# Gate and up with the rows' low parts stacked into the stationary operand, and a fold matmul that sums the halves

## The chip, the cores and the metric

The kernel runs on one core of one Trainium2 chip. The metric is the time on the device in microseconds (us), from three runs of the kernel before; a profile of one further execution gives the rows below.

## The reference, cut to what matters

One layer of a decoder for 512 tokens of 1024 numbers, all in f32: a token mixing stage (retention and a gated linear recurrence), then a mixture of experts (MoE). Each token goes to 2 of 32 experts; an expert has a gate and an up matrix (1024 x 512 each) and a down matrix (512 x 1024).

```python
def expert_rows(args):
    xb, e = args
    h = jax.nn.silu(xb @ w_e_gate[e]) * (xb @ w_e_up[e])
    return h @ w_e_down[e]
```

The results of a token's two experts are weighted and added, and a layer norm ends the layer.

## The kernel before, in words

**Precision.** TensorE multiplies in fp32r, a form of f32 that it takes faster and with fewer bits. To keep more of them each operand is split: the high part is the value rounded to fp32r (a copy by ScalarE), the low part is what is left (a subtraction by VectorE). `products` (line 1402) then issues three matmuls for each block of 128 of the inner dimension: high x high, high x low, low x high (lines 1406, 1407, 1408), all into one PSUM bank.

**The MoE stage.** The kernel goes through the 32 experts in order, with up to 64 rows (tokens) of an expert at a time (`ROWS = 64`). Further rows of an expert are left to an overflow part at the end, which has nothing to do with these inputs. An expert's weights are six units of 1 MB each (128 partitions x 2048 f32): two halves each of gate, up and down, called G0, G1, U0, U1, D0, D1 here. A unit is loaded by SyncE's queue into one of 12 buffers (`m_raw`, `MRING = 12`), rounded by ScalarE into one of 3 buffers of `m_hi` (`m_hi_part`, line 787, which waits until TensorE has finished the unit three before), and completed by VectorE in `m_lo` (`m_lo_part`, line 1329), which also frees the load's buffer. SyncE issues a load when its buffer is free (line 381).

**The rows.** GpSimd gathers the rows of an expert from device memory into `xg` (line 492). TensorE turns them (`turn_x`, line 1618: eight transposes of 64 rows x 128 columns, line 1625), so that the inner dimension lies on the partitions, into PSUM (`bank_x`). ScalarE and VectorE split them into `xe_hi` and `xe_lo` (lines 795 and 1333). These have 128 columns, of which the 64 rows fill the first 64; the others were set to zero once (lines 815 to 817). They are the stationary operands of gate and up (`gate_up`, line 1628): 4 units x 4 blocks x 3 products = 48 matmuls with 512 moving columns, gate into bank 0 and up into bank 1. Only PSUM partitions 0 to 63 of the result mean anything.

**From gate and up to down.** ScalarE takes silu of the gate bank (`silu_part`, line 803, 128x512), VectorE multiplies it with the up bank into `h_sb` (`h_part`, line 1341, 128x512). TensorE turns h (`turn_h`, line 1639, four transposes), ScalarE and VectorE split it into `ht_hi` and `ht_lo` (lines 799 and 1337), and `down` (line 1646) makes 2 units x 2 blocks x 2 halves x 3 products = 24 matmuls into banks 2 and 3. ScalarE copies them out (`y_out`, line 807) and GpSimd scatters the rows to device memory.

**The order** is written out by hand for each engine, and each engine works strictly in its order. In the body for expert e (a loop of 15 turns with two experts in each, then once more for e = 30), with `hi` for `m_hi_part`, `lo` for `m_lo_part`, and 2 to 7 for U0, U1, D0, D1 and the next expert's G0 and G1:

```python
# TensorE, line 1665
gate_up(e + 1, u); turn_x(e + 2); down(e, u.ahead(4)); turn_h(e + 1)
# ScalarE, line 827
hi(2); ht_hi_part(e); hi(3); hi(4); silu_part(e + 1, ..); hi(5); hi(6); xe_hi_part(e + 2); hi(7); y_out(e, ..)
# VectorE, line 1355
lo(2); ht_lo_part(e); lo(3); lo(4); lo(5); h_part(e + 1, ..); lo(6); xe_lo_part(e + 2); lo(7)
```

So gate and up of the next expert run before down of this one. The waits are counts on semaphores: `m_done` (TensorE has finished a unit), `m_hi_ok` and `m_split_ok` (a unit's high part, both parts are there), `xe_turned`, `xe_split`, `m_silu`, `h_ok`, `h_turned`, `ht_hi_ok`, `ht_split`, `y_ok`. Ahead of the loop stand the first rows, and gate and up of expert 0 (lines 1660 to 1663, 812 to 825, 1346 to 1353); behind it down of expert 31 and the final norm. `Unit` (line 74) numbers the units and gives a unit's buffer. Elsewhere in the kernel the router (line 1580) multiplies in plain f32, eight matmuls with 128 stationary and 36 moving columns for each block of 128 tokens, and line 1573 transposes 128x128 blocks of f32.

Of the kernel before, what the change touches and what calls it, by code (L numbers as in the profile page):

```python
# [110 lines left out]
def layer(nc, io, out):  # L111
    ctx = ExitStack()
    with ctx:
# [56 lines left out]
        xe_hi, xe_lo = at("xe_hi", 128, [P, KD, P], F32R), at("xe_lo", 132, [P, KD, P], F32R)  # L170
        xg = at("xg", 136, [P, D])
        y_sb = at("y_sb", 140, [P, D])
        silu, h_sb = at("silu", 144, [P, FE]), at("h_sb", 146, [P, FE])
        ht_hi, ht_lo = at("ht_hi", 148, [P, FE // P, P], F32R), at("ht_lo", 150, [P, FE // P, P], F32R)
        bank_x = bank[:, 4:6, :].rearrange("p b (k n) -> p (b k) n", n=P)
        bank_h = bank[:, 6, :].rearrange("p (k n) -> p k n", n=P)
# [82 lines left out]
        m_silu, h_ok, h_turned, ht_hi_ok, ht_split = sem("m_silu"), sem("h_ok"), sem("h_turned"), sem("ht_hi_ok"), sem("ht_split")  # L259
# [313 lines left out]
        def _(act):  # L573
# [221 lines left out]
            def xe_hi_part(s):  # L795
                act.wait_ge(xe_turned, s + 1)
                copy(xe_hi[:, :, 0:ROWS], bank_x[:, :, 0:ROWS]).then_inc(xe_hi_ok, 1)

            def ht_hi_part(s):
                act.wait_ge(h_turned, s + 1)  # L800
                copy(ht_hi[:, :, 0:ROWS], bank_h[:, :, 0:ROWS]).then_inc(ht_hi_ok, 1)

            def silu_part(s, u):
                m_finished(u)
                act.activation(silu[:, :], bank[:, 0, :], ACT.Silu).then_inc(m_silu, 1)
# [9 lines left out]
            for tile in (xe_hi, xe_lo, ht_hi, ht_lo):  # L815
                n = tile.shape[1]
                act.activation(tile[:, :, ROWS:P], ident[:, 0:P - ROWS].unsqueeze(1).to_broadcast([P, n, P - ROWS]), ACT.Copy, scale=0.0)
# [3 lines left out]
            for j in range(4):  # L821
                if j == 2:
                    silu_part(0, u.ahead(1))
                m_hi_part(u.ahead(j + 2))
            xe_hi_part(1)

            def act_next(e, u):

                m_hi_part(u.ahead(2))
                ht_hi_part(e)  # L830
                m_hi_part(u.ahead(3))
                m_hi_part(u.ahead(4))
                silu_part(e + 1, u.ahead(1))
                m_hi_part(u.ahead(5))
                m_hi_part(u.ahead(6))
                xe_hi_part(e + 2)
                m_hi_part(u.ahead(7))
                y_out(e, u.ahead(5))

# [8 lines left out]
            with act.If(n_over > 0):  # L848
                with act.Fori(0, (MAX_OVERFLOW + 1) // 2) as i:
                    for b in range(2):  # L850
                        j = 2 * i + b
                        with act.If(n_over > j):
# [4 lines left out]
                            silu_part(j + EXPERTS, u.ahead(1))  # L857
# [19 lines left out]
        def _(dve):  # L877
# [448 lines left out]
            dve.tensor_scalar(lists_x[0:ROWS, :], lists[0:ROWS, :], 1, None, ALU.logical_shift_right).then_inc(lists_x_ok, 1)  # L1326

# [5 lines left out]
            def xe_lo_part(s):  # L1333
                dve.wait_ge(xe_hi_ok, s + 1)
                sub(xe_lo[:, :, 0:ROWS], bank_x[:, :, 0:ROWS], xe_hi[:, :, 0:ROWS]).then_inc(xe_split, 1)

            def ht_lo_part(s):
                dve.wait_ge(ht_hi_ok, s + 1)
                sub(ht_lo[:, :, 0:ROWS], bank_h[:, :, 0:ROWS], ht_hi[:, :, 0:ROWS]).then_inc(ht_split, 1)

            def h_part(s, u):
                dve.wait_ge(m_done, u.n + 1 + MSPLIT)
                dve.wait_ge(m_silu, s + 1)
                tt(h_sb[:, :], bank[:, 1, :], silu[:, :], ALU.mult).then_inc(h_ok, 1)
# [7 lines left out]
            h_part(0, u.ahead(3))  # L1352
            xe_lo_part(1)

            def dve_next(e, u):

                m_lo_part(u.ahead(2))
                ht_lo_part(e)
                for j in range(3, 6):
                    m_lo_part(u.ahead(j))  # L1360
                h_part(e + 1, u.ahead(3))
                m_lo_part(u.ahead(6))
                xe_lo_part(e + 2)
                m_lo_part(u.ahead(7))

# [6 lines left out]
            with dve.If(n_over > 0):  # L1372
                with dve.Fori(0, (MAX_OVERFLOW + 1) // 2) as i:
                    for b in range(2):
                        j = 2 * i + b
                        with dve.If(n_over > j):
# [4 lines left out]
                            h_part(j + EXPERTS, u.ahead(3))  # L1381
# [19 lines left out]
        def _(pe):  # L1401
# [216 lines left out]
            def turn_x(s, ahead=0):  # L1618
# [5 lines left out]
                for k in range(KD):  # L1624
                    last = pe.transpose(bank_x[:, k, 0:ROWS], xg[0:ROWS, P * k:P * k + P], ident[0:ROWS, 0:ROWS])  # L1625
                last.then_inc(xe_turned, 1)

            def gate_up(s, u):
                pe.wait_ge(xe_split, s + 1)
                for b in range(2):  # L1630
                    for half in range(2):
# [3 lines left out]
                        products(bank[:, b, :], [(xe_hi[:, 4 * half + k, :], xe_lo[:, 4 * half + k, :],  # L1635
                                                  m_hi[:, sl, FE * k:FE * k + FE], m_lo[:, sl, FE * k:FE * k + FE]) for k in range(4)],
                                 half == 0, half == 1).then_inc(m_done, 1)

            def turn_h(s):
                pe.wait_ge(h_ok, s + 1)  # L1640
                pe.sem_inc(marks, 1)
                for k in range(4):
                    last = pe.transpose(bank_h[:, k, 0:ROWS], h_sb[0:ROWS, P * k:P * k + P], ident[0:ROWS, 0:ROWS])  # L1643
                last.then_inc(h_turned, 1)
# [18 lines left out]
            turn_h(0)  # L1663

            def pe_next(e, u):
# [4 lines left out]
                turn_h(e + 1)  # L1670
# [8 lines left out]
            with pe.If(n_over > 0):  # L1679
                with pe.Fori(0, (MAX_OVERFLOW + 1) // 2) as i:  # L1680
                    for b in range(2):
                        j = 2 * i + b
                        with pe.If(n_over > j):
                            u = Unit(M_END + 6 * b, 0, i, 12, MRING)
                            turn_x(j + (EXPERTS + 1), 1)
                            gate_up(j + EXPERTS + 1, u)
                            turn_h(j + EXPERTS)
# [39 lines left out]
```

## Time and profile before

| | us |
|---|---|
| median of 3 runs | 1469.64 |
| lowest and highest | 1469.45, 1474.08 |
| span of the profiled execution | 1470.0 |
| TensorE busy in it | 1361.7 (93%) |
| VectorE busy | 956.6 (65%) |
| ScalarE busy | 780.9 (53%) |
| GpSimd busy | 205.4 (14%) |

The profiled execution has no time of its own beside its span, which runs from its first to its last instruction; it stands 0.4 us above the median. TensorE has two rows in the profile: PE is the matmuls and transposes, PEld their weight loads, which run beside them. A matmul with 512 moving columns shows some 0.39 us while the next begins 0.227 us after it, since they are pipelined: the distance of starts is what a matmul costs, not its duration. "fp32r" in a row is the split form; the names are the program's with buffer numbers left out. DVE is VectorE, ACT ScalarE, POOL GpSimd.

### The profile page before, as it was taken

The numbers are of one execution on the slowest core, as the hardware profiler recorded it, in microseconds if no ns is written. First come the engines' busy times: TensorE is split into PE (matmuls) and PEld (weight loads), VectorE is DVE, ScalarE is ACT, GpSimd is POOL, SyncE is SP. The second block draws the span as 40 slices with busy tenths as digits, with TensorE's granted clock in tenths as the row PEclk, the third lists the DMA queues.
The fourth block names the chain that finished last, engine by engine and source line by source line (L and its number), as shares of the span: only waits on it lengthen the run. The fifth ranks groups of instructions, "written<-read, shape, count | busy, mean of one in ns | idle before, by whom it ended". The sixth has DMA issues, their size and how long they took to land.

```text
span 1470.0 us, 18266 instructions
## 1 busy us (share of the span) xinstructions
PE 1361.7 (93%) x6264; PEld 1113.0 (76%) x6264; DVE 956.6 (65%) x1013; ACT 780.9 (53%) x768; POOL 205.4 (14%) x177
## 2 busy tenths in 40 slices
PE   7999999999999999999988089999999999999970
PEld 6888878878888888888877067777888888887860
DVE  5478853363734734634654368888888888888857
ACT  5676653223424333334321257777777777777751
POOL 0000000000000000003300312222222222222222
PEclk9999999999999999999998589999999999999995
DMA  7233213523131322332474369999999999999804
GB/s 225 81 90 102 71 58 97 164 74 113 58 114 58 100 85 72 100 86 72 129 272 162 142 212 351 367 370 376 361 357 372 366 370 367 366 374 365 322 13 171
DMA packets 202404, 294.20 MB, mean 200 GB/s; under 512 B 11968, under 2 KB 109424, under 8 KB 201856
## 3 DMA queue, kind: packets, MB, share of 16 engines
q1 hardware_dynamic: 196224, 283.17, 56.2%
q0 software_dynamic: 5568, 8.47, 1.7%
q10 hardware_dynamic: 576, 2.10, 0.4%
q8 instruction: 21, 0.34, 0.1%
q14 instruction: 15, 0.12, 0.0%
HBM read 289.96 MB, written 12.65 MB: 206 GB/s over the span
## 4 chain that ended last, share of the span: by engine, by line
PE 89%; DVE 4%; DMA 2%; ACT 2%; issue 2%; POOL 1%; ACTq 0%; POOLq 0%; DVEq 0%
PE bank L1406 29%; PE bank L1408 28%; PE bank L1407 28%; PE bank L1625 1%; PE bank L1643 1%; PE bank L1580 1%; DVE x L1394 1%; DVE wo_lo L885 1%; DMA list_dram<-val,addr 1%; DMA x_rows<-in_x_dram 0%; PE bank L1508 0%; DMA xg<-x_dram,x_idx 0%; DVE x L1193 0%; POOL list_dram L490 0%; DVE m_lo L885 0%
## 5 line engine op out<-in xcount | busy, mean ns | idle before, releaser
L885 DVE TENSOR_TENSOR m_lo<-m_raw,m_hi 128x2048 fp32r<-128x2048 f32 x192 | 439.4, 2289 | 93.5 <-ACT m_hi L575 93.5
L575 ACT ACTIVATE m_hi<-m_raw 128x2048 fp32r<-128x2048 f32 x192 | 368.1, 1918 | 112.2 <-PE bank L1408 111.7
L885 DVE TENSOR_TENSOR w_lo<-raw,w_hi 128x1024 fp32r<-128x1024 f32 x120 | 148.5, 1239 | 184.6 <-ACT w_hi L575 183.3
L1406 PE MATMUL bank<-xt_hi,w_hi 128*128 128x512 f32 x576 | 225.1, 391 | 2.7 <-ACT merge L664 1.0
L1408 PE MATMUL bank<-xt_hi,w_lo 128*128 128x512 f32 x576 | 224.1, 389 | 0.0
L1407 PE MATMUL bank<-xt_lo,w_hi 128*128 128x512 f32 x576 | 224.1, 389 | 0.0
L575 ACT ACTIVATE w_hi<-raw 128x1024 fp32r<-128x1024 f32 x120 | 126.3, 1058 | 171.9 <-PE bank L1408 171.9
L1406 PE MATMUL bank<-m_hi,xe_hi 128*128 128x512 f32 x512 | 204.2, 399 | 1.6 <-DVE xe_lo L885 1.6
L1408 PE MATMUL bank<-m_hi,xe_lo 128*128 128x512 f32 x512 | 200.9, 392 | 0.0
L1407 PE MATMUL bank<-m_lo,xe_hi 128*128 128x512 f32 x512 | 200.7, 392 | 0.0
L1406 PEld LDWEIGHTS bank<-xt_hi,w_hi 128*128 128x128 f32 x576 | 108.2, 188 | 25.9 <-ACT merge L664 1.5
L1408 PEld LDWEIGHTS bank<-xt_hi,w_lo 128*128 128x128 f32 x576 | 108.1, 188 | 22.5
L1407 PEld LDWEIGHTS bank<-xt_lo,w_hi 128*128 128x128 f32 x576 | 108.2, 188 | 22.0
L1406 PEld LDWEIGHTS bank<-m_hi,xe_hi 128*128 128x128 f32 x512 | 97.0, 190 | 23.2 <-DVE xe_lo L885 1.6
L1408 PEld LDWEIGHTS bank<-m_hi,xe_lo 128*128 128x128 f32 x512 | 96.8, 189 | 20.6
L1407 PEld LDWEIGHTS bank<-m_lo,xe_hi 128*128 128x128 f32 x512 | 97.0, 190 | 19.4
L470 POOL TENSOR_TENSOR acc<-acc,g_ret 128x512 f32<-128x512 f32 x8 | 10.5, 1310 | 689.9 <-ACT g_ret L739 689.9
L1406 PE MATMUL bank<-m_hi,ht_hi 128*128 128x512 f32 x256 | 103.7, 405 | 1.6 <-DVE ht_lo L885 1.6
L1408 PE MATMUL bank<-m_hi,ht_lo 128*128 128x512 f32 x256 | 100.1, 391 | 0.0
L1407 PE MATMUL bank<-m_lo,ht_hi 128*128 128x512 f32 x256 | 99.7, 390 | 0.0
L497 POOL DMA_INDIRECT xg<-x_dram,x_idx x34 | 89.9, 2646 | 26.9 <-POOL x_idx L494 26.9
L494 POOL COPY x_idx<-lists_x 64x1 int32 (+1 forms) x34 | 26.8, 789 | 314.3 <-PE bank L1625 305.1
(240 smaller groups left out, 1994.1 us busy)
## 6 DMA issues: line engine op xcount, KB each, us to landing
m_raw<-in_w_e_gate_dram SPq DMA_DIRECT2D x64, 1024.0 KB, 7.9
m_raw<-in_w_e_up_dram SPq DMA_DIRECT2D x64, 1024.0 KB, 7.3
m_raw<-in_w_e_down_dram SPq DMA_DIRECT2D x64, 1024.0 KB, 7.1
raw<-in_w_in_dram SPq DMA_DIRECT2D x88, 512.0 KB, 4.0
raw<-in_w_ret_o_dram SPq DMA_DIRECT2D x16, 512.0 KB, 3.3
raw<-in_w_lru_o_dram SPq DMA_DIRECT2D x16, 384.0 KB, 3.0
raw<-in_w_out_dram SPq DMA_DIRECT2D x8, 512.0 KB, 3.5
y_rows<-y_dram SPq DMA_DIRECT2D x4, 1024.0 KB, 7.8
```

The source lines that it names most:

```text
L470: steps(pool.tensor_tensor(acc[:, k, :], acc[:, k, :], g_ret[:, k, :], ALU.mult))
L494: steps(pool.tensor_copy(x_idx[0:ROWS, :], lists_x[0:ROWS, ds(col, 1)] if not isinstance(col, int) else lists_x[0:ROWS, col:col + 1]))
L497: pool.indirect_dma_start(xg[0:ROWS, :], None, x2_dram, bass.IndirectOffsetOnAxis(ap=x_idx[0:ROWS, :], axis=0), bounds_check=last_x, oob_i ...
L575: return act.activation(dst, src, ACT.Copy)
L885: return dve.tensor_tensor(dst, a, b_r.bitcast(F32), ALU.subtract)
L1394: step(dve.scalar_tensor_tensor(x2[:, t, :], y_rows[:, t, D * k:D * k + D], wts[:, 2 * t + k:2 * t + k + 1], x2[:, t, :], ALU.mult, ALU.add))
L1406: pe.matmul(dst, sh, mh, start=first and x == 0, stop=False)
L1407: pe.matmul(dst, sh, ml, start=False, stop=False)
L1408: ins = pe.matmul(dst, sl, mh, start=False, stop=last and x == n - 1)
L1580: last = pe.matmul(bank[:, 6, 36 * t:36 * t + 36], x2_t[:, t % 2, P * k:P * k + P], w_rt[:, 36 * k:36 * k + 36], start=k == 0, stop=k == K ...
L1625: last = pe.transpose(bank_x[:, k, 0:ROWS], xg[0:ROWS, P * k:P * k + P], ident[0:ROWS, 0:ROWS])
L1643: last = pe.transpose(bank_h[:, k, 0:ROWS], h_sb[0:ROWS, P * k:P * k + P], ident[0:ROWS, 0:ROWS])
```

## The change

The low parts of the rows go into the empty columns 64 to 127 of the same stationary tile: `xe` has the high parts in columns 0 to 63 and the low parts in 64 to 127. A product of `xe` with `m_hi` gives high x high in partitions 0 to 63 of the bank and low x high in 64 to 127; a product with `m_lo` adds high x low, and also low x low, to the same halves. So `gate_up` issues two matmuls for each block, not three. The two halves of the bank must then be added: ScalarE copies the gate bank (`gate_evict`) and VectorE the up bank (`up_evict`) into `gu_sb`, and TensorE multiplies each block of 128 columns of `gu_sb` (stationary, plain f32) with `fold`, two 64x64 identities on top of each other (`fold_gu`, eight matmuls with 64 moving columns). That adds the halves and turns the result at once, so the turn of h is gone, and silu and h are taken on the turned form, 128 partitions x 256 elements each. `ht_hi` and `ht_lo` are split from `h_t` in SBUF, not from PSUM.

The order changes too: in the bodies of ScalarE and VectorE `ht_hi_part` and `ht_lo_part` move ahead of the split of unit 2 (U0); `silu_part` and `h_part` move to the end, behind `y_out` and behind the split of unit 7; `gate_evict` and `up_evict` stand where silu and h stood. The diff, cut (semaphores and the overflow part are left out, the latter has the same changes):

```diff
-        xe_hi, xe_lo = at("xe_hi", 128, [P, KD, P], F32R), at("xe_lo", 132, [P, KD, P], F32R)
-        xg = at("xg", 136, [P, D])
-        y_sb = at("y_sb", 140, [P, D])
-        silu, h_sb = at("silu", 144, [P, FE]), at("h_sb", 146, [P, FE])
+        xe = at("xe", 128, [P, KD, P], F32R)
+        xg = at("xg", 132, [P, D])
+        y_sb = at("y_sb", 136, [P, D])
+        gu_sb = at("gu_sb", 140, [P, 2, FE])
+        silu, h_t = at("silu", 144, [P, FE // P, ROWS]), at("h_t", 145, [P, FE // P, ROWS])
+        fold = at("fold", 146, [P, ROWS])
         ht_hi, ht_lo = at("ht_hi", 148, [P, FE // P, P], F32R), at("ht_lo", 150, [P, FE // P, P], F32R)
-        bank_x = bank[:, 4:6, :].rearrange("p b (k n) -> p (b k) n", n=P)
-        bank_h = bank[:, 6, :].rearrange("p (k n) -> p k n", n=P)
+        bank_x = bank[:, 4, :].rearrange("p (k n) -> p k n", n=ROWS)
+        bank_t = bank[:, 5, :].rearrange("p (b k n) -> p b k n", b=2, n=ROWS)
...
             def xe_hi_part(s):
                 act.wait_ge(xe_turned, s + 1)
-                copy(xe_hi[:, :, 0:ROWS], bank_x[:, :, 0:ROWS]).then_inc(xe_hi_ok, 1)
+                copy(xe[:, :, 0:ROWS], bank_x[:, :, :]).then_inc(xe_hi_ok, 1)
 
             def ht_hi_part(s):
-                act.wait_ge(h_turned, s + 1)
-                copy(ht_hi[:, :, 0:ROWS], bank_h[:, :, 0:ROWS]).then_inc(ht_hi_ok, 1)
-
-            def silu_part(s, u):
+                act.wait_ge(h_ok, s + 1)
+                copy(ht_hi[:, :, 0:ROWS], h_t[:, :, :]).then_inc(ht_hi_ok, 1)
+
+            def gate_evict(u):
                 m_finished(u)
-                act.activation(silu[:, :], bank[:, 0, :], ACT.Silu).then_inc(m_silu, 1)
+                copy(gu_sb[:, 0, :], bank[:, 0, :]).then_inc(gate_out, 1)
+
+            def silu_part(s):
+                act.wait_ge(folded, s + 1)
+                act.activation(silu[:, :, :], bank_t[:, 0, :, :], ACT.Silu).then_inc(m_silu, 1)
...
-            for tile in (xe_hi, xe_lo, ht_hi, ht_lo):
+            for tile in (ht_hi, ht_lo):
...
                 if j == 2:
-                    silu_part(0, u.ahead(1))
+                    gate_evict(u.ahead(1))
                 m_hi_part(u.ahead(j + 2))
             xe_hi_part(1)
+            silu_part(0)
 
             def act_next(e, u):
 
+                ht_hi_part(e)
                 m_hi_part(u.ahead(2))
-                ht_hi_part(e)
                 m_hi_part(u.ahead(3))
                 m_hi_part(u.ahead(4))
-                silu_part(e + 1, u.ahead(1))
+                gate_evict(u.ahead(1))
                 m_hi_part(u.ahead(5))
                 m_hi_part(u.ahead(6))
                 xe_hi_part(e + 2)
                 m_hi_part(u.ahead(7))
                 y_out(e, u.ahead(5))
+                silu_part(e + 1)
...
+            dve.tensor_copy(fold[0:ROWS, :], ident[0:ROWS, 0:ROWS]).then_inc(fold_ok, 1)
+            dve.tensor_copy(fold[ROWS:P, :], ident[ROWS:P, ROWS:P]).then_inc(fold_ok, 1)
...
             def xe_lo_part(s):
                 dve.wait_ge(xe_hi_ok, s + 1)
-                sub(xe_lo[:, :, 0:ROWS], bank_x[:, :, 0:ROWS], xe_hi[:, :, 0:ROWS]).then_inc(xe_split, 1)
+                sub(xe[:, :, ROWS:P], bank_x[:, :, :], xe[:, :, 0:ROWS]).then_inc(xe_split, 1)
 
             def ht_lo_part(s):
                 dve.wait_ge(ht_hi_ok, s + 1)
-                sub(ht_lo[:, :, 0:ROWS], bank_h[:, :, 0:ROWS], ht_hi[:, :, 0:ROWS]).then_inc(ht_split, 1)
-
-            def h_part(s, u):
+                sub(ht_lo[:, :, 0:ROWS], h_t[:, :, :], ht_hi[:, :, 0:ROWS]).then_inc(ht_split, 1)
+
+            def up_evict(u):
                 dve.wait_ge(m_done, u.n + 1 + MSPLIT)
+                dve.tensor_copy(gu_sb[:, 1, :], bank[:, 1, :]).then_inc(up_out, 1)
+
+            def h_part(s):
                 dve.wait_ge(m_silu, s + 1)
-                tt(h_sb[:, :], bank[:, 1, :], silu[:, :], ALU.mult).then_inc(h_ok, 1)
+                tt(h_t[:, :, :], bank_t[:, 1, :, :], silu[:, :, :], ALU.mult).then_inc(h_ok, 1)
...
-            h_part(0, u.ahead(3))
             xe_lo_part(1)
+            up_evict(u.ahead(3))
+            h_part(0)
 
             def dve_next(e, u):
 
-                m_lo_part(u.ahead(2))
                 ht_lo_part(e)
-                for j in range(3, 6):
+                for j in range(2, 6):
                     m_lo_part(u.ahead(j))
-                h_part(e + 1, u.ahead(3))
+                up_evict(u.ahead(3))
                 m_lo_part(u.ahead(6))
                 xe_lo_part(e + 2)
                 m_lo_part(u.ahead(7))
+                h_part(e + 1)
...
-                for b in range(2):
+                for b, out_sem in enumerate((gate_out, up_out)):
+                    if not (isinstance(s, int) and s == 0):
+                        pe.wait_ge(out_sem, s - ahead if ahead else s)
                     for half in range(2):
                         v = u.ahead(2 * b + half)
                         pe.wait_ge(m_split_ok, v.n + 1 + MRING)
                         sl = v.slot % MSPLIT
-                        products(bank[:, b, :], [(xe_hi[:, 4 * half + k, :], xe_lo[:, 4 * half + k, :],
-                                                  m_hi[:, sl, FE * k:FE * k + FE], m_lo[:, sl, FE * k:FE * k + FE]) for k in range(4)],
-                                 half == 0, half == 1).then_inc(m_done, 1)
-
-            def turn_h(s):
-                pe.wait_ge(h_ok, s + 1)
-                pe.sem_inc(marks, 1)
-                for k in range(4):
-                    last = pe.transpose(bank_h[:, k, 0:ROWS], h_sb[0:ROWS, P * k:P * k + P], ident[0:ROWS, 0:ROWS])
-                last.then_inc(h_turned, 1)
+                        for k in range(4):
+                            pe.matmul(bank[:, b, :], xe[:, 4 * half + k, :], m_hi[:, sl, FE * k:FE * k + FE], start=half == 0 and k == 0, stop=False)
+                            last = pe.matmul(bank[:, b, :], xe[:, 4 * half + k, :], m_lo[:, sl, FE * k:FE * k + FE],
+                                             start=False, stop=half == 1 and k == 3)
+                        last.then_inc(m_done, 1)
+
+            def fold_gu(s):
+                pe.wait_ge(gate_out, s + 1)
+                pe.wait_ge(up_out, s + 1)
+                for b in range(2):
+                    for k in range(FE // P):
+                        last = pe.matmul(bank_t[:, b, k, :], gu_sb[:, b, P * k:P * k + P], fold[:, :], start=True, stop=True)
+                last.then_inc(folded, 1)
...
-            turn_h(0)
+            pe.wait_ge(fold_ok, 2)
+            fold_gu(0)
...
                 gate_up(e + 1, u)
                 turn_x(e + 2)
                 down(e, u.ahead(4))
-                turn_h(e + 1)
+                fold_gu(e + 1)
```

## Rows read from the trace of the kernel before

**Rows 1.** The page: TensorE's granted clock in 40 slices of the span

```profile
PEclk9999999999999999999998589999999999999995
```

**Rows 2.** Table of stretches: busy us by engine, PEclk, DMA share, GB/s

```profile
750.00:770.00 20.00, 20.00 (x93) 16.60 (x93) 8.36 (x16) 1.24 (x2) 0.00 (x0) 1.00 1.04 408
...
1312.76:1384.06 71.30, 71.30 (x337) 57.02 (x337) 60.41 (x37) 54.68 (x41) 18.92 (x16) 1.00 1.03 374
```

**Rows 3.** The chain that ended last: start us, us, what

```profile
847.59 0.61 ACT xe_hi L575
848.22 0.70 DVE xe_lo L885
848.97 0.80 PE bank L1406
...
878.20 0.64 PE bank L1625 x8
...
1395.17 0.64 PE bank L1625 x8
```

**Rows 4.** Timeline of TensorE's matmuls around the two turns of one expert

```profile
1109.56 0.39 PE L1408 MATMUL bank<-m_hi,xe_lo 128*128 128x512 f32 x1
1109.88 0.71 PE L1625 MATMUL bank<-ident,xg 64*128 64x64 f32 x8
1110.51 0.50 PE L1406 MATMUL bank<-m_hi,ht_hi 128*128 128x512 f32 x1
...
1115.88 0.39 PE L1408 MATMUL bank<-m_hi,ht_lo 128*128 128x512 f32 x1
1116.20 0.46 PE L1643 MATMUL bank<-ident,h_sb 64*128 64x64 f32 x4
1116.59 0.50 PE L1406 MATMUL bank<-m_hi,xe_hi 128*128 128x512 f32 x1
1116.93 0.39 PE L1407 MATMUL bank<-m_lo,xe_hi 128*128 128x512 f32 x1
```

**Rows 5.** Timeline of router and transposes: matmuls, then weight loads (PEld)

```profile
792.15 1.87 PE L1580 MATMUL bank<-w_rt,x_t 128*128 128x36 f32 x16
793.85 1.07 PE L1573 MATMUL bank<-ident,x 128*128 128x128 f32 x8
...
793.74 0.94 PEld L1573 LDWEIGHTS bank<-ident,x 128*128 128x128 f32 x8
```

**Rows 6.** Groups of instructions, 878 to 1395 us: busy us, mean ns

```profile
L885 DVE TENSOR_TENSOR m_lo<-m_raw,m_hi 128x2048 fp32r<-128x2048 f32 x175 | 400.7, 2290 | 79.4 <-ACT m_hi L575 79.4
L575 ACT ACTIVATE m_hi<-m_raw 128x2048 fp32r<-128x2048 f32 x174 | 333.9, 1919 | 97.4 <-PE bank L1408 96.9 <-issue 0.5
...
L885 DVE TENSOR_TENSOR xe_lo<-bank,xe_hi 128x512 fp32r<-128x512 f32 x29 | 19.9, 685 | 0.0
...
L885 DVE TENSOR_TENSOR ht_lo<-bank,ht_hi 128x256 fp32r<-128x256 f32 x29 | 12.1, 418 | 0.0
L575 ACT ACTIVATE ht_hi<-bank 128x256 fp32r<-128x256 f32 x29 | 10.8, 372 | 0.0
```

**Rows 7.** Timeline of VectorE, two instructions that follow without a wait

```profile
1119.17 2.29 DVE L885 TENSOR_TENSOR m_lo<-m_raw,m_hi 128x2048 fp32r<-128x2048 f32 x1 [1.33 <-ACT m_hi L575]
1121.38 0.42 DVE L885 TENSOR_TENSOR ht_lo<-bank,ht_hi 128x256 fp32r<-128x256 f32 x1
```

**Rows 8.** Pauses of TensorE: stretches around them, and its timeline

```profile
863.20:866.60 3.40, 1.61 (x9) 1.34 (x10) 3.40 (x4) 2.25 (x3) 1.90 (x2) 1.00 0.99 314
866.60:870.00 3.40, 3.40 (x9) 2.70 (x9) 1.22 (x2) 0.09 (x1) 0.00 (x0) 0.51 0.96 340
...
1419.60:1423.00 3.40, 1.78 (x9) 1.41 (x8) 1.68 (x2) 1.06 (x2) 1.38 (x2) 1.00 0.00 0
...
864.83 0.43 PE L1643 MATMUL bank<-ident,h_sb 64*128 64x64 f32 x4 [2.20 <-DVE h_sb L881]
...
1421.33 0.50 PE L1406 MATMUL bank<-m_hi,ht_hi 128*128 128x512 f32 x1 [1.62 <-DVE ht_lo L885]
```

More of the change, by code:

```diff
@@ L258, in layer @@
         xg_in, xe_turned, xe_hi_ok, xe_split = sem("xg_in"), sem("xe_turned"), sem("xe_hi_ok"), sem("xe_split")
-        m_silu, h_ok, h_turned, ht_hi_ok, ht_split = sem("m_silu"), sem("h_ok"), sem("h_turned"), sem("ht_hi_ok"), sem("ht_split")
+        m_silu, h_ok, folded, ht_hi_ok, ht_split = sem("m_silu"), sem("h_ok"), sem("folded"), sem("ht_hi_ok"), sem("ht_split")
+        gate_out, up_out, fold_ok = sem("gate_out"), sem("up_out"), sem("fold_ok")
         y_ok, y_sent, y_free, marks, lists_x_ok = sem("y_ok"), sem("y_sent"), sem("y_free"), sem("marks"), sem("lists_x_ok")
@@ L856, in _ @@
                                 m_hi_part(u.ahead(k))
-                            silu_part(j + EXPERTS, u.ahead(1))
+                            gate_evict(u.ahead(1))
+                            silu_part(j + EXPERTS)
                             ht_hi_part(j + EXPERTS)
@@ L1380, in _ @@
                                 m_lo_part(u.ahead(k))
-                            h_part(j + EXPERTS, u.ahead(3))
+                            up_evict(u.ahead(3))
+                            h_part(j + EXPERTS)
                             ht_lo_part(j + EXPERTS)
@@ L1624, in turn_x, with gate_up @@
                 for k in range(KD):
-                    last = pe.transpose(bank_x[:, k, 0:ROWS], xg[0:ROWS, P * k:P * k + P], ident[0:ROWS, 0:ROWS])
+                    last = pe.transpose(bank_x[:, k, :], xg[0:ROWS, P * k:P * k + P], ident[0:ROWS, 0:ROWS])
                 last.then_inc(xe_turned, 1)
-            def gate_up(s, u):
+            def gate_up(s, u, ahead=0):
                 pe.wait_ge(xe_split, s + 1)
-                for b in range(2):
+                for b, out_sem in enumerate((gate_out, up_out)):
+                    if not (isinstance(s, int) and s == 0):
+                        pe.wait_ge(out_sem, s - ahead if ahead else s)
                     for half in range(2):
@@ L1685, in _ @@
                             turn_x(j + (EXPERTS + 1), 1)
-                            gate_up(j + EXPERTS + 1, u)
-                            turn_h(j + EXPERTS)
+                            gate_up(j + EXPERTS + 1, u, 1)
+                            fold_gu(j + EXPERTS)
                             down(j + EXPERTS, u.ahead(4))
```

## The prediction, made before the changed kernel ran

> **What bounds the kernel now.** I read the page's clock slices first: TensorE stays at its upper level, 2.4 GHz, in the mixture-of-experts (MoE) stage, which fills the last 40% of the span [rows 1]. The table of stretches then shows who is full there: TensorE is busy 71.30 of 71.30 us, VectorE 60.41, ScalarE 54.68, and the core moves 374 GB/s [rows 2]. The chain that ended last puts the same x turn (the transposes of the gathered tokens) at 878.20 and 1395.17, 29 experts apart: 17.83 us per expert, all on TensorE [rows 3]. One expert is 72 matmuls at a spacing of 0.227 us (16.3 us), the x turn, which makes 0.95 us of one step between matmuls, and the turn of h [rows 4].
>
> Is something else just behind? Loads: 374 GB/s times 17.83 us is 6.67 MB per expert; the same queue reached 408 GB/s in another stretch [rows 2], so loads alone need 16.3 us. VectorE: six splits, ht_lo, h, xe_lo, 15.1 us busy of 17.83. So both lie within 15% of TensorE, and what matters is not the work of an engine but the order in which three engines hand an expert round.
>
> **What the change does to TensorE's own work.** Gate and up go from 48 to 32 matmuls: minus 16 x 0.227 = 3.63 us. The turn of h (0.39 us from its start to the next matmul [rows 4]) goes. The fold comes: 8 plain f32 matmuls with 128 stationary columns and 64 moving ones. The router shows that a plain f32 matmul is issued as two instructions: 8 products a half appear as 16, starting from 792.15 to 793.85, 0.106 us each with 36 moving columns; and eight 128x128 f32 transposes load weights in 0.94 us, which is (0.94 - 0.19) / 7 = 0.107 each with 128 moving columns [rows 5]. With 36 columns in two passes and with 128 in one the spacing is the same, so the weight load sets it. I take 0.107 for the fold's 16 instructions: 1.71 us. TensorE's own sum is 17.83 - 3.63 - 0.39 + 1.81 = 15.6 us. Were it still the bound, 30 experts would give 66 us back.
>
> **A rule against that price.** Rows 5 say 0.107 us. The Trainium skill, TensorE: Matmul & The Clock Gate, "Back-to-back issue gap", gives about 81 ns per matmul for a stream of weight load and matmul pairs at 128 columns. By that rule the fold would last 1.3 us. The 64-partition transposes of x [rows 4] do run at 0.080 us, so it isn't idle; it is a rival below, worked out from that row.
>
> **The new loop.** The old order let ScalarE split U0 (first half of up; G, U, D name gate, up, down halves) before it took ht_hi. Now ScalarE and VectorE begin an expert with ht_hi and ht_lo, and U0's split is queued behind ht_hi. ht_hi waits for h_part, that for silu, that for the fold, and the fold stands behind down on TensorE. The ring closes: h, ht_hi, split of U0 and U1, up's second half, x turn, down, fold, silu, h. I walk it from the end of h_part = 0, durations from [rows 6], 0.03 us from ScalarE to VectorE (847.59 + 0.61 to 848.22) and from TensorE to ScalarE, 0.05 for the others (848.22 + 0.70 to 848.97) [rows 3], and 0.08 us by which an instruction overlaps the one before it (2.29 us long, 2.21 apart [rows 7]):
> - ht_hi 0.05 to 0.42; m_hi of U0 0.34 to 2.26 (1.92); m_lo of U0 2.29 to 4.58; m_lo of U1 4.50 to 6.79.
> - TensorE, U1: 6.85; first step 0.34, six of 0.227: last start 8.55. The step over the x turn is 0.95 (1109.56 to 1110.51): down starts 9.50. Down's 24 matmuls take 5.37 to their last start (1110.51 to 1115.88): 14.87. Step to the fold 0.32: 15.19 [rows 4].
> - Fold: 15 x 0.107 = 1.61, last start 16.80, its end 0.28 later (the router's 16 take 1.87, less 15 x 0.106): 17.08.
> - silu on half the elements, 0.37: 17.11 to 17.48. h_part on half, 0.42: 17.51 to 17.93.
>
> So the period is 17.93 us, 0.10 longer than now. The 3.63 us that TensorE saves appear as a pause instead: after G0 and G1 it waits for U0 from about 2.8 to 4.6, 1.8 us, and 0.3 before U1.
>
> The other parts of the change lie beside that ring. gate_evict on ScalarE and up_evict on VectorE (both sized by xe_lo, which reads as much PSUM: 0.69, spacing 0.60) run while TensorE does down; h on half the elements costs 0.42 for 0.69, so silu and h together pay most of them back. VectorE in order: 2.29, 4.50, 6.71, 8.92 (D1), 11.13 (up_evict), 11.73, 13.94 (xe_lo), 14.54 (G1), free at 16.75; h_part could end at 17.17. That is VectorE's floor, and its cover for up_evict is 0.76 us. y_out comes before silu on ScalarE, but ends at 16.3. The split of D1 waits for U0's matmuls and ends at 11.2, before its use at 12.2. The next expert's G0 and G1 are ready at 16.8, just as the fold ends. Loads are issued when VectorE frees a slot, two experts ahead; at 17.9 us they have 1.6 us of slack. GpSimd's gather still follows the x turn, 17 us before its use. The fill of xe's empty half is gone (two 0.6 us copies), hidden under the wait for the first gather; two copies into the fold tile cost VectorE well under a microsecond in that same wait: nothing.
>
> **Start and end.** First expert: its matmuls start at 848.97 at half clock [rows 3], where nine of them fill 3.4 us, 0.43 apart [rows 8]; ScalarE's fourth split waits for the first unit, which is now 8 matmuls, not 12: minus 1.7, and so on down the same walk, to a fold at 862.9 (behind up_evict), h_part's end at 865.6 and the x turn 8.9 later at 874.5, against 878.20 now: minus 3.7. A pause of 3.0 us ahead of this fold will probably lower the clock for a while (see below), so I take minus 2.8; ends minus 3.7 and minus 1. Last expert: from the start of down(30)'s last matmul to down(31) it is now 0.32 to the turn, 0.46 for it and the pause of 1.62 [rows 4, 8] = 2.40 us; in the new order 0.32 + 1.61 + 0.28 + silu, h, ht_hi, ht_lo with their steps 1.76 = 3.97: plus 1.6.
>
> **Sum.** Against the profiled execution's span of 1470.0 us (0.4 above the median of 1469.64): 30 x 0.10 - 2.8 + 1.6 = +1.8, so 1472 us. The unknown sizes: the steps between engines and the 256-element operations, some ten on the ring at 0.02 each, give 0.2 per period, 6 us; that makes 1464 to 1480 for this case. About 0.3% (4.4 us) is what a measurement can tell from no change.
>
> **Rivals.**
> - *The clock falls (slower).* The pause of 1.8 us before U0 now comes once per expert. In the trace a stretch with a 2.20 us pause was followed by 0.51 of the clock for 3.4 us, a stretch with a 1.62 us pause by the full clock [rows 8]. The point lies between them. 3.4 us at 0.43 for 0.227 loses 1.6 us of U0, U1 or down, all on the ring. In half the periods: 15 x 1.6 = 24, 1496 us; in all of them 1520. For: the pause is new. Against: it is nearer to the harmless one. Chance 0.15.
> - *The fold pays load and columns in turn (slower).* 64 columns in two passes at the rate of 512 in 0.227 would add 0.057 for a pass of 128 cycles: 15 x 0.057 x 30 = 26, 1497 us. Against: equal spacing at 36 and at 128 columns. Chance 0.06. It is also the upper end of the fold's price.
> - *Cheaper weight loads (faster).* At the x turn's 0.080 the fold's steps shrink by 15 x 0.027 = 0.40: period 17.53, 1460 us. (By the skill's 81 ns the same.) For: the x turn's row. Against: it loads 64 partitions, the fold 128. Chance 0.10.
> - *A fold that costs nearly nothing (faster).* At 0.03 a step VectorE's floor of 17.17 sets the period: 30 x (17.17 - 17.93) = -23, 1449 us. Chance 0.07; it is the fold's lower end.
> - *TensorE stays the bound (faster).* If U0's split did not wait behind ht_hi, the period would be VectorE's or TensorE's work, 15.6 us: about 1404 us. The order in the code excludes it unless I misread a queue. Chance 0.04.
>
> **Chances.** Forecast 0.58, of which 0.08 ends faster than 0.3%, 0.27 within, 0.23 slower. With the rivals: faster 0.08 + 0.10 + 0.07 + 0.04 = 0.29; same 0.27; slower 0.23 + 0.15 + 0.06 = 0.44. The range 1450 to 1494 leaves out the bound on TensorE, half of the nearly free fold, the upper part of the clock case and of the costly fold: 0.18 in all.
>
> **What would show it.** In the profile after, the distance between two x turns should be 17.9 us. TensorE should be busy about 88% of the MoE stage, with a pause before each up product, released by VectorE's m_lo, in total some 1.8 x 30 = 54 us. ScalarE's m_hi or ht_hi should wait for VectorE's h_t, h_t for silu, silu for the fold. The fold's 16 instructions should start 0.107 apart, the granted clock should stay 1.00 from the second expert on, and up_evict should be released by TensorE or by nothing. A period near 15.6 would say that the ring does not exist; one near 17.2 that VectorE's queue is the bound; a clock below 1.00 in the stage that the pause is too long. If the fold's instructions stand 0.16 apart, the price of a plain f32 matmul was read wrongly.

## The result and the profile after

The changed kernel takes 1482.46 us (median; 1481.53 to 1487.19) against 1469.89 us of the kernel before on the same chip: ratio 1.0084, 95% interval 1.0061 to 1.0106. It is slower by 12.6 us. The range held it, the forecast value of 1472 was 10 us low. The profiled execution is the slowest of the four: its span is 1485.5 us, 15.5 more than the one of before, while the other three have spans of 1479.8 to 1480.9 and a mean granted clock of 0.953 to 0.954 for its 0.950. What is counted below is counted in it; the others probably had some four falls of the clock fewer (an estimate: 4.9 us by the 1.2 us that one fall costs).

The page of the changed kernel, engines' share and slices, and the group of the fold:

```profile
PE 1323.6 (89%) x6136; PEld 1079.1 (73%) x6136; DVE 968.9 (65%) x1047; ACT 788.6 (53%) x798; POOL 216.6 (15%) x177
...
PEclk9999999999999999999997589999999999999985
...
L1665 PE MATMUL bank<-fold,gu_sb 128*128 128x64 f32 x512 | 61.9, 275 | 3.4 <-DVE gu_sb L1355 3.4
```

TensorE does less (1361.7 us busy before) and the kernel takes longer. The fold has 512 instructions, 16 per expert. In the slices the clock looks as in [rows 1], because a slice of 37 us hides a short fall; the table of stretches shows it. Columns as in [rows 2]:

```profile
900.00:1300.00 400.00, 359.37 (x1739) 284.21 (x1739) 337.43 (x219) 305.14 (x241) 112.47 (x87) 0.97 0.99 356
955.50:973.40 17.90, 16.02 (x82) 12.62 (x81) 15.43 (x10) 13.96 (x11) 5.41 (x5) 1.00 1.01 372
```

From 900 to 1300 us TensorE is busy 90% and gets 0.97 of its clock; in one undisturbed expert it gets all of it. The chain that ended last shows one such expert (start us, us, what):

```profile
952.91 1.69 PE bank L1665 x15
954.62 0.40 ACT silu L812
955.04 0.44 DVE h_t L891
955.50 0.04 ACT ht_hi L578
...
955.82 1.91 ACT m_hi L578
957.75 0.06 DVE m_lo L895
957.81 1.76 issue
...
959.96 2.30 DVE m_lo L895
...
962.30 0.50 PE bank L1655
...
964.44 0.64 PE bank L1642 x8
965.08 0.43 PE bank L1423
...
970.77 1.75 PE bank L1665 x16
972.54 0.39 ACT silu L812
```

Before, this chain was TensorE from end to end [rows 3]. Now it goes round three engines: fold, silu, h, ht_hi, m_hi and m_lo of U0, m_lo of U1 (959.96), up's second half, x turn, down, fold. From silu to silu it takes 17.92 us. (The piece called "issue" at 957.81 is no wait: VectorE works at m_lo of U0 from 957.75 to the start of U1's.) Meanwhile TensorE waits. Its timeline has in brackets the idle time and its releaser; behind it stand the waits in 878 to 1395 us, which are short but come once per expert (engine, line, releaser: us in total, times, longest):

```profile
923.12 0.50 PE L1655 MATMUL bank<-m_hi,xe 128*128 128x512 f32 x1 [1.79 <-DVE m_lo L895]
```

```profile
PE bank L1655 <- DVE m_lo L895: 50.1, 28, 1.8
...
ACT silu L812 <- PE bank L1665: 20.5, 29, 0.7
DVE h_t L891 <- ACT silu L812: 17.4, 28, 0.6
ACT ht_hi L578 <- DVE h_t L891: 13.8, 28, 0.5
```

After some of these pauses the clock falls. Stretches around the pause that ends at 923.12:

```profile
921.20:924.60 3.40, 1.61 (x7) 1.23 (x7) 3.40 (x2) 3.40 (x3) 0.00 (x0) 0.99 0.93 360
924.60:928.00 3.40, 3.40 (x9) 2.50 (x8) 3.17 (x3) 2.13 (x2) 0.00 (x0) 0.51 0.94 335
```

They read like the first pair of [rows 8]. From 887 to 1420 us there are 12 such stretches at 1.2 GHz, called low stretches below, 3.4 us each; they come every second or third expert, though the pause is 1.79 us in all of them but the last (1.88). A fold follows the one before it by 17.9 us at full clock and by 19.1 us where a low stretch lies between (915.87 to 934.98 in the chain).

**The account.** The x turn stands at 872.47, and 30 experts later at 1423.80: 18.38 us each, 17.83 before. That is 30 x 0.08 = 2.4 us of longer ring and 12 x 1.2 = 14.3 of clock. The first gather arrived 4.0 us sooner (842.50 for 846.47) and the start after it is 1.8 us shorter. The end is 4.6 us longer: 1.6 between the last x turn and down(31), and 3.1 because down(31) ran in a low stretch of 6.8 us. 2.4 + 14.3 - 4.0 - 1.8 + 4.6 = 15.5.

### The profile page after: what moved, and what is told of

Its sections match the earlier page's. It is cut to its first block, busy times and chain, and to the rows that moved or that the text cites. A ratio compares the mean times of both kernels' runs of the same rounds, so it can differ in the third digit from the quotient of the medians.

```text
span 1485.5 us, 18073 instructions
## 1 busy us (share of the span) xinstructions
PE 1323.6 (89%) x6136; PEld 1079.1 (73%) x6136; DVE 968.9 (65%) x1047; ACT 788.6 (53%) x798; POOL 216.6 (15%) x177
## 4 chain that ended last, share of the span: by engine, by line
PE 76%; DVE 10%; ACT 6%; issue 5%; DMA 2%; POOL 0%; ACTq 0%; DVEq 0%; POOLq 0%
PE bank L1423 21%; PE bank L1425 20%; PE bank L1424 20%; DVE m_lo L895 5%; PE bank L1655 4%; ACT m_hi L578 4%; PE bank L1665 4%; PE bank L1656 4%; PE bank L1642 1%; DVE h_t L891 1%; ACT silu L812 1%; PE bank L1597 1%; DVE x L1411 1%; DVE wo_lo L895 1%; DMA x_rows<-in_x_dram 1%
## 5 line engine op out<-in xcount | busy, mean ns | idle before, releaser
L895 DVE TENSOR_TENSOR m_lo<-m_raw,m_hi 128x2048 fp32r<-128x2048 f32 x192 | 432.4, 2288 | 59.4 <-ACT m_hi L578 59.2
L578 ACT ACTIVATE m_hi<-m_raw 128x2048 fp32r<-128x2048 f32 x192 | 360.5, 1908 | 77.7 <-PE bank L1656 40.3
L1655 PE MATMUL bank<-m_hi,xe 128*128 128x512 f32 x512 | 222.9, 435 | 57.4 <-DVE m_lo L895 54.3
L1656 PE MATMUL bank<-m_lo,xe 128*128 128x512 f32 x512 | 214.2, 418 | 0.0
L1655 PEld LDWEIGHTS bank<-m_hi,xe 128*128 128x128 f32 x512 | 104.5, 204 | 101.6 <-DVE m_lo L895 76.5
L1656 PEld LDWEIGHTS bank<-m_lo,xe 128*128 128x128 f32 x512 | 104.6, 204 | 21.0
L497 POOL COPY x_idx<-lists_x 64x1 int32 (+1 forms) x34 | 36.0, 1058 | 326.8 <-PE bank L1642 318.7
L1665 PEld LDWEIGHTS bank<-fold,gu_sb 128*128 128x128 f32 x512 | 63.2, 195 | 5.9 <-issue 3.5
L1665 PE MATMUL bank<-fold,gu_sb 128*128 128x64 f32 x512 | 61.9, 275 | 3.4 <-DVE gu_sb L1355 3.4
```

The costliest lines, as they stand in the source:

```text
L497: steps(pool.tensor_copy(x_idx[0:ROWS, :], lists_x[0:ROWS, ds(col, 1)] if not isinstance(col, int) else lists_x[0:ROWS, col:col + 1]))
L578: return act.activation(dst, src, ACT.Copy)
L895: return dve.tensor_tensor(dst, a, b_r.bitcast(F32), ALU.subtract)
L1655: pe.matmul(bank[:, b, :], xe[:, 4 * half + k, :], m_hi[:, sl, FE * k:FE * k + FE], start=half == 0 and k == 0, stop=False)
L1656: last = pe.matmul(bank[:, b, :], xe[:, 4 * half + k, :], m_lo[:, sl, FE * k:FE * k + FE], start=False, stop=half == 1 and k == 3)
L1665: last = pe.matmul(bank_t[:, b, k, :], gu_sb[:, b, P * k:P * k + P], fold[:, :], start=True, stop=True)
```

## The experiments

Times are medians; every ratio is to the kernel before on the same chip, whose median was 1471.97, 1472.46, 1472.52 and 1472.18 us in the four sets. The period is the time of one expert, read from two x turns (or two splits of xe) far apart without a low stretch between them.

### Does the pause cost only through the clock?

Eight more matmuls fill the pause, and one more shortens it.

```diff
                         last.then_inc(m_done, 1)
+                    if b == 0:
+                        for k in range(8):          # 1 in the second kernel
+                            pe.matmul(bank[:, 6, :], xe[:, k, :], xe[:, 0:4, :], start=True, stop=True)
```

> The changed kernel with eight more matmuls of 512 columns (xe with xe, into an unused bank, nobody reads them) between the gate and the up products of every expert, where TensorE pauses 1.79 us. They last 8 x 0.227 = 1.8 us. Theory (the ring sets the period, and the pause makes the clock fall): the period at full clock stays 17.90 us although TensorE has 1.8 us more to do, no stretch at the lower level is left from the second expert on, and the 12 or so longer periods (19.1 us for 17.9) go: 1482.5 - 14 = 1468 us. Rival (TensorE's work sets the time): 31 x 1.8 = 56 us more, 1538. Rival (the falls cost nothing, something else makes the long periods): 1482.

> As the filled pause, but with one extra matmul instead of eight: the pause ahead of the up products shrinks from 1.79 to about 1.56 us. Theory by the length of the pause (1.62 us was harmless in the kernel before, 1.79 not always): no falls, all periods 17.90 us, 1469 us. Rival (what counts is how much TensorE does around the pause, and a quarter of a microsecond changes little): still about a dozen low stretches, 1480 us.

Measured: eight 1471.45 us, ratio 0.9998 (0.9988 to 1.0007); one 1471.19 us, ratio 0.9991 (0.9982 to 1.0001). Period 17.88 and 17.89 us, and 17.90 in the changed kernel. In the loop there is no low stretch in either. The eight, the stretch with them, and the pause that one left:

```profile
957.91 1.98 PE L1661 MATMUL bank<-xe 128*128 128x512 f32 x8
```

```profile
900.00:1300.00 400.00, 398.05 (x1969) 316.40 (x1969) 342.81 (x225) 312.64 (x248) 120.10 (x90) 1.00 1.01 366
```

```profile
956.51 0.50 PE L1655 MATMUL bank<-m_hi,xe 128*128 128x512 f32 x1 [1.56 <-DVE m_lo L895]
```

TensorE does 1.8 us more per expert, is busy 398 of 400 us for 359, and the kernel is faster than the changed one by 0.9% of the time before. So TensorE's work is not the bound, and the falls are what made 1482 of some 1470. In this order a quarter of a microsecond less pause was enough; another order is below whose pauses are shorter still and whose clock falls.

### What lies on the ring?

The same eight matmuls behind up's products:

```diff
                         last.then_inc(m_done, 1)
+                for k in range(8):
+                    pe.matmul(bank[:, 6, :], xe[:, k, :], xe[:, 0:4, :], start=True, stop=True)
```

> The same eight extra matmuls as in the filled pause (1.8 us per expert, into an unused bank), but behind the up products, ahead of the x turn. Theory (U1 to down to the fold lie on the ring, gate does not): the period grows by the whole 1.81 us, 17.90 to 19.7, and the pause of 1.8 us ahead of up stays, so falls of the clock too: 1470 + 54 = 1524 us without falls, up to 1540 with them. Rival (TensorE has 1.8 us to spare anywhere in the period): 1470 to 1482 us, as when they stood ahead of up.

Measured: 1549.96 us, ratio 1.0521 (1.0503 to 1.0540). Period 19.70 us at full clock (folds at 1025.23 and 1044.93 in its chain), and 19 low stretches in the loop, some 1.2 us each. That is 10 us above the upper end of what was expected, since that end allowed 16 us for falls and 19 of them cost 23. The same work costs nothing at one place and 1.8 us at the other: the forecast's order of events holds. By that order it can also be said where the 16 dropped matmuls were worth something, which no run shows apart: four stood in U1 on the ring, and the eight in gate only lengthened the pause.

The fold with half the instructions:

```diff
-        gu_sb = at("gu_sb", 140, [P, 2, FE])
+        gu_sb = at("gu_sb", 140, [P, 2, FE], F32R)
-        fold = at("fold", 146, [P, ROWS])
+        fold = at("fold", 146, [P, ROWS], F32R)
```

> The changed kernel with gu_sb and the fold tile in fp32r: gate and up are rounded to fp32r before the fold (that precision is left out), and the fold is 8 matmul instructions, not 16. Theory: 8 x 0.107 = 0.86 us less on the ring, period 17.05 to 17.2 (VectorE's floor), the pause of 1.8 us stays and so do the falls of the clock: 1482.5 - 30 x 0.75 = 1460 us. Rival (the fold lies beside the ring): 1482.

Measured: 1456.23 us, ratio 0.9892 (0.9876 to 0.9909). Period 17.17 us at full clock, the prediction's floor for VectorE: h follows VectorE's last split without a wait. In that floor VectorE still stands idle for 1.8 us per expert, until ht_hi and m_hi of U0 are there. The fold is on the ring. The clock falls 8 times in the loop. TensorE's pause reads 1.98 to 2.17 us, longer than in the changed kernel, with fewer falls: the length of the pause alone does not say how often the clock falls.

```profile
952.45 0.50 PE L1655 MATMUL bank<-m_hi,xe 128*128 128x512 f32 x1 [1.99 <-DVE m_lo L895]
```

### Is it the order?

First the move of ht_hi and ht_lo alone, both ways: undone in the changed kernel, and made in the kernel before.

```diff
 # ScalarE; VectorE's ht_lo_part and split of u.ahead(2) alike
-                ht_hi_part(e)
                 m_hi_part(u.ahead(2))
+                ht_hi_part(e)
```

> The changed kernel with one part of its reordering undone: ScalarE's and VectorE's split of U0 stands ahead of ht_hi and ht_lo again; silu and h stay at the end. Theory (ring through h, ht_hi, split of U0): m_hi of U0 starts when silu ends, not when ht_hi does; the end of U1's m_lo comes 0.6 us earlier, period 17.3 us, the pause before the up products shrinks from 1.8 to some 0.9 us and the clock stays up: 1482.5 - 14 - 30 x 0.6 = 1450 us. Rival (the order of ht_hi is harmless, the fold's place alone costs): within 3 us of 1482.

> The kernel before with only the move of ht_hi and ht_lo ahead of the split of U0 (three products, turn of h, silu and h where they were). Theory (the move costs only because silu and h stand behind the fold): h is ready before down ends, so ht_hi follows the turn of h at once, m_lo of U0 ends some 4.7 us after gate begins and is needed at 5.4: no change, 1470 us within 3. Rival (ht_hi ahead of U0's split delays up whatever stands before it): period up by 0.5 us or more, 1485 us.

Measured: undone 1456.42 us, ratio 0.9889 (0.9872 to 0.9905), period 17.38 us, pauses of 0.88 and 1.01 us in turn, no low stretch in the loop. Made in the kernel before, 1472.46 us, ratio 1.0002 (0.9993 to 1.0012), period 17.83. The move costs 0.5 us per expert where silu and h stand behind the fold, and nothing where they don't. What made the change slower is thus the pair: h waits for the fold, and U0's split waits for h.

Then both splits of up ahead of what hangs on the fold:

```diff
 # ScalarE; VectorE alike with m_lo_part, ht_lo_part, h_part
             def act_next(e, u, more=True):
+                m_hi_part(u.ahead(3))
                 ht_hi_part(e)
-                m_hi_part(u.ahead(2))
-                m_hi_part(u.ahead(3))
...
                 y_out(e, u.ahead(5))
+                if more:
+                    m_hi_part(u.ahead(8))
                 silu_part(e + 1)
```

> The changed kernel with another order on ScalarE and VectorE: the split of U0 stands ahead of silu and h, the split of U1 ahead of ht_hi and ht_lo. So no split of gate or up waits for the fold. Theory: the ring is cut, TensorE pauses at most 0.6 us per expert, and the period falls to the larger of TensorE's work (15.6 plus small pauses) and the loads' 16.3 us: 16.3 to 16.7 us, 1470 - 1 - 30 x 1.35 = 1428 us, between 1420 and 1436, clock full. Rival (VectorE's work with its waits is the bound): 17.2 us, 1449. Rival (the fold matmul itself is too dear): no faster than before, 1470.

Measured: 1426.73 us, ratio 0.9692 (0.9676 to 0.9708), period 16.43 us, no low stretch in the loop. It beats both kernels with the same arithmetic as the change. That TensorE is near its bound here follows from the next kernel, which has 16 matmuls per expert more:

```diff
                         for k in range(4):
+                            pe.matmul(bank[:, 6, :], xe[:, 4 * half + k, :], m_hi[:, sl, FE * k:FE * k + FE], start=True, stop=True)
                             pe.matmul(bank[:, b, :], xe[:, 4 * half + k, :], m_hi[:, sl, FE * k:FE * k + FE], ...)
```

> The order with U0's split ahead of silu, and a third matmul for each block of gate and up again (16 more per expert, into an unused bank), so that TensorE has the work it had in the kernel before, plus the fold for the turn of h. Theory: with the ring cut TensorE becomes the bound and the products count in full: 15.6 + 3.63 = 19.2 us per expert, 1427 + 30 x 2.8 = 1511 us. Rival (the products dropped were never worth much): below 1470.

Measured: 1506.94 us, ratio 1.0238 (1.0221 to 1.0255), period 19.03 us. With the ring cut, dropping the products is worth 2.6 us per expert, 80 us in all. In the change as made nearly all of that went into the pause.

### What bounds the better order?

> The order with U0's split ahead of silu, and the fold in fp32r (gate and up rounded before the fold; that precision is left out). In that order the ring runs from down's end over y_out, m_hi and m_lo of U0, h, m_lo of U1, U1, x turn and down, and no longer over the fold. Theory: the period stays 16.43 us although TensorE has 0.86 us less to do: 1427 us, within 4. Rival (TensorE's work is the bound there): period 15.6, 1402 us.

> The order with U0's split ahead of silu, and y_out moved behind that split on ScalarE. In the run with that order VectorE idled 1.08 us per expert ahead of m_lo of U0, which waited for m_hi, which stood behind y_out (1.02 us). Theory (y_out is on what is left of the ring): the gap shrinks to 0.2 us; VectorE could then go at 15.6 us per expert, but the loads need 6.56 MB / 408 GB/s = 16.1 us: period 16.1, 1426.7 - 10 = 1417 us, between 1404 and 1420. Rival (the loads already bound the 16.43 us, at 399 GB/s): 1426 us.

The first has the two fp32r lines from above. The second moves one line:

```diff
-                y_out(e, u.ahead(5))
                 if more:
                     m_hi_part(u.ahead(8))
+                y_out(e, u.ahead(5))
                 silu_part(e + 1)
```

Measured: the short fold 1418.89 us, ratio 0.9634 (0.9618 to 0.9651), period 16.21; the late y_out 1427.44 us, ratio 0.9693 (0.9677 to 0.9709), period 16.40. Neither expectation fits. The short fold was to give nothing and gave 0.2 us per expert; the late y_out was to give 0.3 and gave nothing. VectorE's timelines say why. In the order above, and then with the late y_out:

```profile
1030.07 2.29 DVE L897 TENSOR_TENSOR m_lo<-m_raw,m_hi 128x2048 fp32r<-128x2048 f32 x1 [1.08 <-ACT m_hi L578]
1032.28 0.42 DVE L893 TENSOR_TENSOR h_t<-bank,silu 128x256 f32<-128x256 f32 x1
1032.79 2.29 DVE L897 TENSOR_TENSOR m_lo<-m_raw,m_hi 128x2048 fp32r<-128x2048 f32 x1
```

```profile
1027.64 4.69 DVE L897 TENSOR_TENSOR m_lo<-m_raw,m_hi 128x2048 fp32r<-128x2048 f32 x2
1032.25 0.42 DVE L893 TENSOR_TENSOR h_t<-bank,silu 128x256 f32<-128x256 f32 x1
1033.68 2.29 DVE L897 TENSOR_TENSOR m_lo<-m_raw,m_hi 128x2048 fp32r<-128x2048 f32 x1 [1.02 <-ACT m_hi L578]
```

The gap of a microsecond moved from U0's split to U1's. There m_hi waits for one of three buffers, which G0's products free, and these stand behind the fold (some 0.5 us per expert in ScalarE's waits, released by TensorE's L1662). So two rings of nearly the same length were left. Both were then shortened at once, and another way round was tried: G0's products ahead of the fold, both of up's splits ahead of silu, y_out last.

```diff
 # TensorE
-                gate_up(e + 1, u)
+                gate_up(e + 1, u, units=(1, 2, 3))
                 turn_x(e + 2)
                 down(e, u.ahead(4))
+                if more:
+                    gate_up(e + 2, u.ahead(6), units=(0,))
                 fold_gu(e + 1)
 # ScalarE; VectorE alike
                 m_hi_part(u.ahead(7))
-                y_out(e, u.ahead(5))
+                if more:
+                    m_hi_part(u.ahead(8))
+                    m_hi_part(u.ahead(9))
                 silu_part(e + 1)
+                y_out(e, u.ahead(5))
```

> The last order (y_out behind U0's split) with the fold in fp32r (gate and up rounded before the fold). Theory after the last runs: two rings of nearly the same length were left, one over y_out and the split of U0 (16.22 us, seen with the short fold), one over the fold, the G0 products, and the split of U1, which waits for the buffer that G0 frees (16.4 us, seen with the late y_out). Shortening either alone gave 8 us or nothing. With both short the period falls to what the loads allow, 6.56 MB / 408 GB/s = 16.1 us, or if they can go faster to TensorE's 15.6: 1417 us down to 1402. Rival (the loads bound it at 403 GB/s already): 1419 us, no better than the short fold alone.

> Full precision, no change of the arithmetic: TensorE takes the next expert's G0 products ahead of the fold, ScalarE and VectorE split U0 and U1 ahead of silu and h, y_out stands last. So the buffer that U1's split waits for comes free 1.7 us earlier and neither the fold nor y_out is on a ring with the splits. Theory: same bound as with both links short, 16.1 us by the loads or 15.6 by TensorE: 1417 to 1402 us. Rival (silu and h now come so late that down waits for ht_lo): a pause ahead of down's first product, period above 16.4, 1427 us or more.

Measured: both short 1404.78 us, ratio 0.9545 (0.9531 to 0.9559), period 15.75, the fastest of the study, with gate and up rounded to fp32r before the fold. G0 ahead of the fold 1451.47 us, ratio 0.9869 (0.9847 to 0.9891), period 17.20, with three falls of the clock in the loop: its rival came true. The table of stretches for both short and a row of its ScalarE near the end; then a TensorE row, a wait, and the stretches around one fall of the other:

```profile
900.00:1300.00 400.00, 377.24 (x1827) 297.36 (x1826) 387.31 (x254) 345.49 (x279) 220.05 (x102) 1.00 1.04 402
```

```profile
1318.72 1.92 ACT L578 ACTIVATE m_hi<-m_raw 128x2048 fp32r<-128x2048 f32 x1 [0.81 <-DMA m_raw<-in_w_e_gate_dram]
```

```profile
1025.78 0.50 PE L1431 MATMUL bank<-m_hi,ht_hi 128*128 128x512 f32 x1 [1.43 <-DVE m_lo L898]
```

```profile
ACT ht_hi L578 <- DVE h_t L894: 37.5, 23, 1.9
```

```profile
900.40:903.80 3.40, 1.97 (x15) 1.33 (x13) 2.35 (x2) 3.40 (x4) 1.55 (x2) 1.00 1.05 409
903.80:907.20 3.40, 3.40 (x11) 2.72 (x12) 3.40 (x3) 2.18 (x2) 2.29 (x1) 0.69 1.05 396
```

Shortened one by one the two rings gave 8 us and nothing, together 22. VectorE is busy 387 of 400 us there and is the likely bound up to 1290 us; this was not tested apart. The loads were a bound all the same, only a late one. In the other kernels GB/s times period gives 6.53 to 6.56 MB per expert (399 x 16.43, 403 x 16.21, 367 x 17.83). Here 402 x 15.75 is 6.33 MB: the kernel used up loads faster than they came, some 5 MB in 25 experts, out of the lead that its 12 buffers give. A load took 9.4 to 10.2 us from issue to landing around 920 us and 15.0 to 16.8 around 1270, and from 1293 us on ScalarE waits for loads; of the last three periods two are longer, 16.17 and 17.36 us. At 402 to 406 GB/s the loads allow 16.1 to 16.3 us per expert in the long run, so 15.75 us would not have lasted through many more experts.

G0 ahead of the fold built a new ring of the old kind: ScalarE waited for h again, now with D0's split queued behind it, and down paused 1.43 us. Three of these pauses were followed by a fall (rows above, for the pause that ended at 903.80), though they are shorter than the 1.56 us that left the clock alone in all 30 experts of the other order.

## Why the prediction was right, and where not

**The ring.** Right in kind and in size. Forecast 17.93 us, measured 17.9; the pause before up forecast at 1.8 us, measured 1.79; the fold's 16 instructions forecast at 1.71 us, measured 1.70 from its start to the next matmul (915.71 to 917.41). The eight extra matmuls behind up against ahead of it, 1.81 us against nothing, show that this is the cause and no coincidence of sums.

**The fold's price.** Right: two instructions for each plain f32 matmul, 0.106 us apart. That the weight load sets this spacing is argued from its being the same with 36, 64 and 128 moving columns; no run varied the weight load. The Trainium skill (TensorE: Matmul & The Clock Gate, "Back-to-back issue gap") gives about 81 ns for 128 moving columns. This case's f32 transposes with 128 columns took 0.107 us [rows 5], so the figure does not hold here and the measurement decides. The three rivals about the fold's price fell with it.

**The clock.** This is the step that failed, and it is why the value was low. The prediction took the harmless case as the likelier, because 1.8 us lay nearer to a pause of 1.62 us without a fall than to one of 2.20 us with one. At 1.79 us the clock fell in 12 of 30 experts, at 1.56 us in none, and in another order at 1.43 us in 3: a pause's length between two rows was no ground for a chance of 0.15. The rival was priced at 1.6 us for each fall; it cost 1.2. In the expert with the rows above, eight slow steps cost 8 x 0.2 = 1.6 us, but some 0.4 of that was the short wait ahead of U1 that an undisturbed expert has anyway (its step there is 0.48 us, and the next 0.35, where others are 0.23); the prediction had that wait, "0.3 before U1", and did not set it off. Put together for the profiled execution: the forecast's 1471.8, less 0.6 in the ring, plus 14.3 for falls, less 4.0 for the first gather, plus 1.0 for the rest of the start, plus 3.1 for the fall at the end, gives 1485.6. The range held the time because the rival's price was in it; and it was luck that the first gather and the fall at the end, neither of them foreseen, cancelled within a microsecond.

**TensorE stays the bound.** It did not. Its number, 15.6 us of own work per expert, can be checked on the kernel with three products and the fold, where TensorE is busy 400 of 400 us: 19.03 us measured for 15.6 + 3.63 = 19.2 reckoned. A slip is part of the difference: the sum has 1.81 us for the fold, where its own price is 1.71, so it should read 15.5.

**VectorE's floor** of 17.17 us came out as the period with the short fold, 17.17. It is a floor of this order only, since it contains the wait for ht_hi and m_hi of U0; other orders ran at 16.43 and 15.75 us. **The loads' limit** of 16.3 us (16.1 in the later expectations) was undercut for 27 experts at 15.75 us, on the lead of the buffers, and then showed. It did not matter for the forecast.

**Start and end.** Forecast minus 2.8, measured minus 1.8 from the first gather on; forecast plus 1.6, measured plus 1.6, and 3.1 more because the clock also fell at the pause ahead of the last down, which was left out. That pause is 1.84 us in the changed kernel and with one extra matmul, where the clock fell, and also with eight, where it did not. Why the first gather came 4.0 us sooner was not tried. It landed at 846.5 and 846.8 us in the two profiles of the old arithmetic, at 841.1 to 844.0 in eleven of the twelve with the new one, and at 846.1 in the twelfth, so it is not one execution's chance alone.

## What to carry to other kernels

Work taken from the busiest engine is a gain only if nothing else stands in the loop that its results travel. Write the loop down as one chain from an instruction to its own next turn, with each engine's queue as links, and add it up; here that gave 17.93 us where the engine's own sum said 15.6. When a stage is moved behind a new step, look at what its engine has queued after it: an independent split behind a waiting ht_hi alone cost 0.5 us per expert.

Two rings of nearly equal length hide each other: shortening one does little, and the other shows only then. A freed engine that now pauses can lose its clock; a run that fills the pause tells how much of the time is that. A period shorter than the loads can follow runs for a while on the buffers' lead: look at whether the time from issue to landing grows.

## What was not expected of the hardware

One extra matmul of 0.227 us per expert made the kernel 0.9% faster (ratio 0.9991 for 1.0084): with pauses of 1.56 us the clock stayed at 2.4 GHz, and with 1.79 us it fell in 12 of 30 cases. The length of a pause does not settle it alone. At the same 1.79 us and a period of 19.7 us it fell in 19 of 30, with pauses of 2.0 to 2.2 us and a period of 17.2 us in 8, and with 1.43 us and nearly the same period in 3. What does settle it was not found.
